# The input projection by 7 block products in place of 8, with the sums of weight blocks beside the delta rule on VectorE

## The reference

```python
proj = hn @ w_in                    # 2048 -> 9232 columns
q, k, v, z, b_logit, a_logit, p, gate_a, gate_b = jnp.split(proj, split_idx, axis=-1)
qkv = silu(causal_dwconv(concatenate([q, k, v]), conv_w))       # 4 taps
o = gated_delta_rule_chunked(q, k, v, beta, g)                  # 8 heads of 128
y_a = (rms(o) * o_norm_w * silu(z)) @ w_proj_a
y_b = (causal_multiscale_pool(p) @ pool_w * pool_scale) @ w_proj_b   # windows 2, 4, 8, 16
merged = sigmoid(gate_a) * y_a + sigmoid(gate_b) * y_b
x = x + merged @ w_out
x = x + (silu(hn2 @ w_gate) * (hn2 @ w_up)) @ w_down            # 2048 -> 5632 -> 2048
```

## Time and profile before

| | |
|---|---|
| median of 3 runs | 2724.44 us (2724.24 to 2725.61) |
| span of the profiled execution | 2722.7 us |
| TensorE busy | 2651.1 us, 97% |
| VectorE busy | 1835.8 us, 67% |
| ScalarE busy | 998.4 us, 37% |
| GpSimd busy | 341.3 us, 13% |
| second unit of the projection begins | 70.4 us |
| delta rule, first half to last | 332.0 to 860.4 us, one half 65.7 us |
| first merge product | 1054.3 us |

### The profile page before, as it was taken

How to read it: one execution, slowest core, us unless ns; L and a number is a source line. 1 busy time by engine, 2 the same in 40 slices (tenths; PEclk the granted TensorE clock), 3 DMA queues, 4 the chain that set the end, 5 groups by cost and what they waited for, 6 DMA issues and landing times.

```text
span 2722.7 us, 44448 instructions
## 1 busy us (share of the span) xinstructions
PE 2651.1 (97%) x17640; PEld 2422.1 (89%) x17640; DVE 1835.8 (67%) x1771; ACT 998.4 (37%) x1025; POOL 341.3 (13%) x350
## 2 busy tenths in 40 slices
PE   8999999999999999998989999999999998999997
PEld 8999988888889987887879999999999996888885
DVE  4444555555553234558888888888888887888886
ACT  4443322222222242223354444444444543333333
POOL 5000044444442420110000000000000000000000
PEclk9999999999999999999999999999999999999998
DMA  4333222223223433778425444545445449756661
GB/s 139 98 92 92 79 78 78 77 77 85 77 77 93 108 93 122 254 241 306 165 97 170 155 150 146 177 152 161 154 154 177 146 141 316 227 194 214 220 213 62
DMA packets 345654, 398.73 MB, mean 146 GB/s; under 512 B 11481, under 2 KB 300386, under 8 KB 344418
## 3 DMA queue, kind: packets, MB, share of 16 engines
q1 hardware_dynamic: 286514, 334.34, 39.1%
q10 hardware_dynamic: 59072, 63.44, 6.8%
HBM read 325.92 MB, written 71.83 MB: 146 GB/s over the span
## 4 chain that ended last, share of the span: by engine, by line
PE 92%; DVE 3%; issue 2%; DMA 1%; ACT 1%; POOL 0%; SPq 0%; DVEq 0%; ACTq 0%; POOLq 0%
PE psum L1973 34%; PE psum L2285 10%; PE psum L2283 10%; PE psum L2284 10%; PE psum L2260 6%; PE psum L2261 6%; PE psum L2262 6%; PE psum L2133 2%; PE psum L2128 1%; PE psum L1922 1%; PE psum L1950 1%; DMA w_raw<-in_w_proj_a 1%; PE psum L2112 1%; PE psum L2205 1%; DVE hq L1630 0%
## 5 line engine op out<-in xcount | busy, mean ns | idle before, releaser
L1973 PE MATMUL psum<-hn_hi,w_hi 128*128 128x264 f32 (+1 forms) x1600 | 450.4, 330 | 0.0
L1973 PE MATMUL psum<-hn_hi,w_lo 128*128 128x264 f32 (+1 forms) x1600 | 449.6, 330 | 0.0
L1973 PE MATMUL psum<-hn_lo,w_hi 128*128 128x264 f32 (+1 forms) x1600 | 449.4, 330 | 0.0
L1296 DVE TENSOR_TENSOR w_lo<-w_raw,w_hi 128x1024 fp32r<-128x1024 f32 x144 | 186.9, 1299 | 253.8 <-ACT w_hi L892 253.4
L1973 PEld LDWEIGHTS psum<-hn_lo,w_hi 128*128 128x128 f32 x1600 | 269.0, 188 | 22.7 <-issue 0.7
L1973 PEld LDWEIGHTS psum<-hn_hi,w_lo 128*128 128x128 f32 x1600 | 268.6, 188 | 22.5
L1973 PEld LDWEIGHTS psum<-hn_hi,w_hi 128*128 128x128 f32 x1600 | 269.0, 188 | 22.0 <-issue 0.2
L892 ACT ACTIVATE w_hi<-w_raw 128x1024 fp32r<-128x1024 f32 x144 | 152.0, 1057 | 371.9 <-PE psum L1973 345.5
L2260 PE MATMUL psum<-dn_hi,act_hl 128*128 128x512 f32 x616 | 242.3, 393 | 15.8 <-DVE hq L1630 14.6
L2261 PE MATMUL psum<-dn_lo,act_hl 128*128 128x512 f32 x616 | 241.5, 392 | 0.0
L2262 PE MATMUL psum<-dn_hi,act_hl 128*128 128x512 f32 x616 | 241.3, 392 | 0.0
(11 more groups left out here) (352 smaller groups left out, 6318.1 us busy)
## 6 DMA issues: line engine op xcount, KB each, us to landing
w_raw<-in_w_in SPq DMA_DIRECT2D x144, 512.0 KB, 3.9
ffn_raw<-in_w_ffn_gate SPq DMA_DIRECT2D x44, 1024.0 KB, 6.4
ffn_raw<-in_w_ffn_up SPq DMA_DIRECT2D x44, 1024.0 KB, 6.5
dn_raw<-in_w_ffn_down SPq DMA_DIRECT2D x40, 1024.0 KB, 7.3
act_hl<-act_dram SPq DMA_DIRECT2D x70, 512.0 KB, 9.3
act_dram<-comb_hi ACTq DMA_DIRECT2D x22, 896.0 KB, 4.2
act_dram<-comb_lo ACTq DMA_DIRECT2D x22, 896.0 KB, 6.2
out_raw<-in_w_out SPq DMA_DIRECT2D x16, 1024.0 KB, 9.7
```

The costliest lines, as they stand in the source:

```text
L1296: dve.tensor_tensor(wlo[s][:], raw[s][:], whi[s][:].bitcast(F32), ALU.subtract).then_inc(S["lo_ready"], 1)
L1973: ins = pe.matmul(o, lhs, r, start=kt == 0 and i == 0, stop=kt == 4 * n_chunks - 1 and i == 2)
```

## The change

The projection `W^T X` is cut in 2 x 2 blocks: the 2048 features in two halves of 1024, a unit's 256 columns in two of 128, the tokens in two of 264 (8 meta and 256 real). Seven products of blocks take the place of eight, by the scheme of Winograd with its four sums on each side. What follows for each engine:

- **Operands.** `hn_hi` and `hn_lo` go; in their place stand seven operands (three blocks of x and the four sums S1 to S4), high and low, [128, 8, 264] each. The sums are made once on VectorE (`operand_sums`).
- **TensorE.** A product is 8 k-tiles x 3, 24 matmuls of 264 columns (K, V, P, Q) or 256 (Z, gates); a unit has 168 (`unit_products`). The logits take 80 matmuls in place of 64. `PIECE` is 14.
- **Weights.** Two loads of 1 MB a unit. VectorE makes `pair_sum`, two block sums in one instruction of 2,048 elements; then `two_sum` and a four-sum, 1,024 each. These two are made by GpSimd for the 20 units before the delta rule and by VectorE for the 16 beside it. ScalarE makes 7 high parts a unit, VectorE 7 low parts, of 1,024 elements each, in place of 4.
- **Results.** ScalarE evicts four quarters of a unit and VectorE combines three times (`combine`, L1665, 256 columns, and L1663, the 8 meta columns).
- **Order of units.** K, V, P, Q and Z all come before the delta rule, 20 units, and the 16 gate units beside it. Results of K, V, Q, the pooled P and SiLU of Z are stored to DRAM and loaded back where they are wanted. The first tap of the convolution moves to ScalarE; the windows of P run on GpSimd during the units behind P's. Behind the delta rule only the zb products stand before the merge.

The core of the diff:

```diff
+PRODUCTS = 7
+BODY = N_GATES // CH
+PIECE = BODY * PRODUCTS * 24 // (2 * STEPS)
...
-                for c in range(4):
-                    load(G_GATES + 4 * u + c, c, w_in_v[:, c:KT:4, bass.ds(COL_GATES + UNIT * u, UNIT)], 4)
...
+            def operand_sums(part):
...
+                dve.tensor_tensor(s1, y21, y22, ALU.subtract).then_inc(S["x_sums"], 1)
+                dve.wait_ge(S["x_sums"], base + 1)
+                dve.tensor_tensor(s2, s1, y11, ALU.subtract).then_inc(S["x_sums"], 1)
+                dve.tensor_tensor(s3, y11, y21, ALU.subtract).then_inc(S["x_sums"], 1)
+                dve.wait_ge(S["x_sums"], base + 2)
+                dve.tensor_tensor(s4, s2, y12, ALU.add).then_inc(S["x_sums"], 1)
...
+            def pair_sums(x):
...
+                dve.tensor_tensor(pair_sum[:], both_b, b12.unsqueeze(1).broadcast_to([P, 2, HEADS, P]), ALU.add) \
+                    .then_inc(S["pairs_done"], 1)
...
+            def sum_two(x):
+                dve.wait_ge(S["pairs_done"], x.u + 1)
+                dve.tensor_tensor(two_sum[:], pair_sum[:, 0], weight_of(x, 5), ALU.add).then_inc(S["twos_done"], 1)
+            def sum_four(x):
+                dve.wait_ge(S["twos_done"], x.u + 1)
+                dve.wait_ge(S["lo_ready"], x.item(1) + 1)
+                dve.tensor_tensor(weight_of(x, 6), two_sum[:], weight_of(x, 1), ALU.add).then_inc(S["fours_done"], 1)
...
+            def unit_event(x, ahead, q, sums=False):
+                a, b, c = x.banks()
+                if q == 0:
+                    weight_low(x, 2)
+                    weight_low(x, 3)
+                elif q == 1:
+                    dve.wait_ge(S["chunk_used"], x.item(1) + 1)
+                    combine(x, b, 0, 0, "sum", 3 * x.u + 1)
+                    weight_low(x, 4)
+                elif q == 2:
+                    weight_low(x, 5)
+                elif q == 3:
+                    weight_low(x, 6)
+                elif q == 4:
+                    dve.wait_ge(S["chunk_used"], x.item(4) + 1)
+                    combine(x, a, 1, 1, "place", 3 * x.u + 3)
+                    if ahead is not None:
+                        pair_sums(ahead)
+                elif q == 5:
+                    if ahead is not None:
+                        weight_low(ahead, 0)
+                        weight_low(ahead, 1)
+                    dve.wait_ge(S["chunk_used"], x.item(5) + 1)
+                    combine(x, c, 1, 0, "bank", 3 * x.u + 2)
+                    if ahead is not None and sums:
+                        sum_two(ahead)
+                        sum_four(ahead)
...
+            def unit_products(x, begins=False):
+                a, b, c = x.banks()
+                width = WIDE if x.wide() else QTR
+                for q in range(PRODUCTS):
+                    pe.wait_ge(S["lo_ready"], x.item(q) + 1)
...
+                    for k in range(HEADS):
+                        hi, lo = w_in_hi[x.ring(q)][:, k, :], low_of(x, q)[:, k, :]
+                        for j, (w, t) in enumerate(((hi, s_hi_q), (hi, s_lo_q), (lo, s_hi_q))):
+                            ins = pe.matmul(out, w, t[:, k, 0:width], start=start and k == 0 and j == 0,
+                                            stop=stop and k == HEADS - 1 and j == 2, skip_group_check=True)
...
-            with pe.Fori(0, N_POOL) as u:
-            with pe.Fori(0, N_Z - 1) as u:
-                z_unit(u)
```

More of the change, by code:

```diff
@@ L496, in _, with in_load @@
                 sp.sem_inc(S[name], count)
+            def in_load(x):
+                if not (isinstance(x.u, int) and x.u < 2):
+                    sp.wait_ge(S["chunk_used"], x.item(0) - PRODUCTS)
+                if x.kind() < N_FIRST:
+                    cols = slice(x.column(), x.column() + UNIT)
+                elif isinstance(x.u, int):
+                    cols = slice(COL_GATES + UNIT * (x.u - N_FIRST), COL_GATES + UNIT * (x.u - N_FIRST + 1))
+                else:
+                    cols = bass.ds(COL_GATES + UNIT * (x.u - N_FIRST), UNIT)
+                for half in range(2):
+                    rows = slice(HEADS * half, HEADS * (half + 1))
+                    sp.dma_start(w_in_raw[x.par()][:, rows, :], w_in_v[:, rows, cols]).then_inc(in_landed[x.par()], 16)
             load_x(0, meta_tokens, META)
@@ L529, in _, with saved_all, stage @@
-            sp.wait_ge(S["gates_stored"], FREE["gates_stored"] + 16 * N_GATES)
-            def merge_unit(u, first):
+            def saved_all(units):
+                for i in range(2):
+                    sp.wait_ge(saved[i], 32 * (units // 2))
+            def stage(n, hf):
+                v, h0 = 2 * n + hf, GH * hf
+                tok = slice(META + P * n, META + P * (n + 1)) if isinstance(n, int) else bass.ds(META + P * n, P)
+                if not (isinstance(v, int) and v == 0):
+                    sp.wait_ge(S["vn_product"], v)
+                for b, t0 in ((7, QT), (8, K_T), (6, VT)):
+                    sp.dma_start(B[b][:], qkv_dram[t0 + h0:t0 + h0 + GH, :, tok].rearrange("h p t -> p h t")) \
+                        .then_inc(S["staged_rows"], 16)
@@ new lines, in _, with gates_beside @@
+            saved_all(Z_U)
+            stage(0, 0)
+            in_load(gate_unit(0, 0))
+            in_load(gate_unit(0, 1))
+            def gates_beside(n, final):
+                for hf in range(2):
+                    for i in range(2 * hf, 2 * hf + 2):
+                        if i < 2:
+                            in_load(gate_unit(n, i + 2))
+                        elif not final:
+                            in_load(chunk_after(n, i - 2))
+                        if i == 0:
+                            stage(n, 1)
+                        elif i == 2 and not final:
+                            stage(n + 1, 0)
@@ L824, in gdn_pool @@
                         level_mask(l + 2)
-                    if l == 3 and following is not None:
-                        stage(*following)
+                    if l == 3 and ahead is not None:
+                        stage(*ahead)
                 pool.wait_ge(S["o_mean"], v + 1)
@@ L908, in _, with conv_event @@
+            def conv_event(x, q):
+                if q in (0, 1) and x.kind() in (K_U, V_U, Q_U):
+                    tap(x, 1 - q)
+                if q in (3, 5):
+                    store(x, 1 if q == 3 else 0)
+            for u in range(2):
                 square_tile(u)
@@ L1320, in _, with conv_event @@
+            def conv_event(x, q):
+                if q in (1, 2):
+                    if x.kind() in (K_U, V_U, Q_U):
+                        taps(x, 2 - q)
+                elif q in (3, 4) and x.kind() == P_U:
+                    pool_tile(x, 4 - q)
             diagonal(0, META)
@@ new lines, in _ @@
+            weigh_x(4)
+            operand_sums(1)
+            weight_low(start, 0)
+            weight_low(start, 1)
+            operand_low(S2, 10)
+            dve.wait_ge(S["x_squared"], TT + 1)
+            for i in range(2):
+                for m in range(2):
+                    dve.memset(conv_in[i][m][:, 0:CONV - 1], 0.0).then_inc(S["set_up"], 1)
+            unit_event(start, first_unit(1), 0)
+            operand_low(S1, 11)
+            operand_low(S3, 12)
+            unit_event(start, first_unit(1), 1)
@@ L2037, in meta_pe @@
+                ins = pe.matmul(PS[:, 6, 2 * HEADS * t:2 * HEADS * (t + 1)], rhs, both[:], start=True, stop=True)
+            ins.then_inc(S["ab_product"], 1)
+            for u in range(2, Z_U):
+                run(unit_products(first_unit(u)))
             def meta_pe():
-                pe.wait_ge(S["meta_staged"], 2)
+                pe.wait_ge(S["meta_landed"], 32)
                 pe.transpose(PS[:, 7, 0:P], m_k, ident[:]).then_inc(S["meta_pe"], 1)
```

1142 lines of the change are left out of this document (692 added, 450 removed).

## The result

The changed kernel takes 2774.14 us, the median of four runs (2771.75 to 2777.78), against 2724.42 us before: 1.0186 times as long, 95% interval 1.0172 to 1.0201. Slower was forecast, by 21.7 us; it is 49.7. The time lies within the whole range (2688 to 2785) but above the forecast's own (2730 to 2762), and the change is more than twice the size that was worked out. The rows of before that each fence answers to are named with it.

The account below looks back on a forecast made before the run. TensorE, almost without waits and fed by VectorE, was taken as the bound. First merge product: 82 + 407 + 6 + 559 + 22 = 1076 us against 1054.3, so +21.7 and 2746 us; range 2730 to 2762, whole range 2688 to 2785.

Parts of the forecast that it names:

- Start-up: Until the second unit begins: first product at 47 to 49 us, second unit at 80.5 to 84, taken as 82.
- Units 2 to 20: Projection units before the delta rule: 381 us of matmuls plus 26 us of waits, 407 in all.
- Matmul price: TensorE's new 256-column matmuls: 0.1167 us each, ends 0.1131 and 0.120, 12 us either way over 20 narrow units.
- A unit's start waits for GpSimd's sum: At a unit's end GpSimd's two-sum blocks VectorE's low part, which ends 1.3 us late, in 16 units.
- Windows: Three units during which GpSimd also makes pooling windows lose some 5 us more between them.
- Delta rule: Each half: 61.5 us of matmuls plus 8.0 of waits, 69.5 in place of 65.7; eight halves 559 us.
- Exclusion: VectorE and GpSimd block each other at SBUF: a delta-rule half takes 69.5 us, the same walk without it 64.9.
- The piece at product 5: In a delta-rule gate unit, VectorE's low parts, combination and sums in one 5.3 us piece; TensorE waits 2.9 us.
- Tail: From the last gate unit to the first merge product: 22 us, bounded by 13.7 and 27.
- Rival 1: VectorE and GpSimd don't collide where it matters, or waits hide: half 64.9, units 381, total 2681 us; chance 0.25.
- Rival 2: VectorE wins the port race at unit ends before the delta rule, halves as forecast: 2720 us, no change; chance 0.13.
- Rival 3: Delta-rule halves worse: pair sums at steps 8 and 20 also delay L1503, 37 us over eight: 2783; chance 0.12.

Follow-up runs that it names:

- the second experiment: Changed kernel with the two-sums and four-sums before the delta rule moved from GpSimd to VectorE: 2745.28 us, 1.0077 times the kernel before.

## Why the prediction was wrong

The step that failed is "Start-up" together with "Units 2 to 20": the sum took the second unit for one like the others. The prediction named GpSimd's two-sum as what a unit's start waits for, but not what stands ahead of the first of them on GpSimd's queue: 38 us of constants, which in the kernel before nobody waited for. The second unit took 32.5 us where 21.5 were in the sum: 7.8 us of waiting and 3 of matmuls on a slow clock behind the wait, 11 us together, removed by moving two instructions. The third and fourth unit stand 3.4 us over the sum: the third ends with a wait of 3.2 us for low parts that stand behind VectorE's work on the logits, and the fourth runs at 0.90 of the clock behind that wait. The sum had no term for the logits' work on VectorE; both excesses stay when the 7.8 us go, so they aren't that wait's. The rest of the 18 us are differences of both signs: 5.4 more for the Z units with the meta step (91.1 for 85.7), 0.6 for the windows, and 2.7 less since seven ordinary units took 21.12 and not 21.5. The statement that the granted clock "stays out of the sum" failed too: it was 0.97 over units 2 to 20, and 0.82 in the worst stretch.

Point by point, the other steps:

- **Matmul price**, 0.1167 with ends at 0.1131 and 0.120: 0.118 in the profile, inside; 264 columns 0.121, where the sum had 0.120. Its cause is open; it isn't the pitch.
- **Start-up**, 82: 84.5. The first product began at 48.3, within 47 to 49.
- **A unit's start waits for GpSimd's sum**, 1.3 us: the mechanism was right, shown by the trace and by the second experiment (units of 20.30 for 21.12). The size was 0.8. With both sums of 20 units moved, the gate units begin 32 us earlier, 11 of these the second unit's, and the time gains 29.
- **Windows**, 5 us more: 5.6 over five units against the forecast's unit of 21.5, 7.6 against the measured one of 21.12. Near.
- **Delta rule**, 69.5 a half: 69.9. The size is right in part by luck. The sum had 61.5 us of work and 8.0 of waits in a half; TensorE was busy for 63.6 and idle for 6.8 (508.7 and 54.0 us over eight), so two misses nearly cancel. The granted clock of 0.98, 1.00 before over the delta rule, is worth 2% of 508.7, some 10 us in all (an estimate), and stood at nothing in the sum. Exclusion is worth at most 2.5 us a half (69.9 to 67.4), forecast 4.6. The piece at product 5 was to take 5.3 us and cost 2.9: it took 6.6 and TensorE's wait behind it was 2.5, as forecast, but with the piece taken apart the half did not shrink, and without any sums it gave 1.2. What counted besides was the pair of low parts in steps 1 to 4: moved, they gave some 2 us.
- **TensorE's jump**: not in the sum at all, 3.0 to 3.3 us in three places, hidden behind VectorE here and worth 4 to 5 us where VectorE is on time.
- **Tail**, 22: 24.0.
- **Rival 1** (61.5 to 65 a half, faster) fell: no run's half came below 67.3 on the mean, also with less work in it. **Rival 2** (VectorE wins the race in every unit) is near to what the second experiment makes by hand; it was priced at 26 us and gave 29, but of the 32 us by which the gate units begin earlier 11 are the queue's and not the race's. **Rival 3** (2783) is nearer to the measured time than the forecast is, but by luck: its halves of some 74 us did not come, 69.9 did.

The Trainium skill ("SBUF — State Buffer", section "Who interferes with whom") has issue order decide who blocks whom. The trace agrees: asking 0.02 us ahead in the changed kernel, GpSimd's two-sum held VectorE's two low parts off for 2.15 of its 2.40 us. That a clean order of the two requests would decide a unit's start was the mechanism forecast, and no run here shows the other order at that place.

Left open: why the delta rule ran at a lower clock, and 9 us longer, once the second unit's wait had gone; what sets the clock in it at all; what makes the Z units and the meta step 5.4 us longer; and what makes 0.118 of 0.113.

## What to carry to other kernels

An instruction that a change makes others wait for has everything ahead of it on its queue as its price: read that queue from its first instruction, also the part that nobody waited for until then. In this kernel, two engines that lock each other out cost least when the sums stood on one of them, even with its busy share at 80%. Work in the way of a chain paid when it moved into an idle piece (two low parts, some 2 us a half) and not when it was only cut up. And a total can come out right over terms that are wrong both ways: compare the busy time and the idle time of the bounding engine with the sum one by one.

## What the runs showed of the hardware

- Masks by `affine_select` on GpSimd took 2.1 to 2.45 us beside VectorE's splits of the operands, where the first two of them took 1.59 and 0.71 us before; the four shown ended 0.4 to 0.6 us behind the VectorE instruction beside which they started.
- A memset of 1,024 float32 a partition on VectorE took 0.91 us, a two-input sum of as many 1.22 us.
- TensorE stood still for 3.0 to 3.3 us at the jump back of a loop with 672 gate matmuls; the loop of before, with 384, showed 0.3 us at most, and written out the loop showed none.
- Behind a wait of 7.8 us TensorE ran at a granted clock of 0.50 (1.2 GHz) from 98.2 to 104.2 us and at 1.00 (2.4 GHz) from 104.4 on, 0.82 on the mean of the 17.5 us.
- Two kernels with the same matmuls in the delta rule (the changed one, and the one with the second unit's sums on VectorE) had TensorE busy for 508.7 and 519.2 us in it, at a granted clock of 0.98 and 0.96.
